# Running the next sequence's scores inside this sequence's softmax waits, in a paged latent-attention decode

## The reference, cut to what matters

```python
past_ckv = cache_ckv[page_table].reshape(db, -1, MLA_KV_RANK)     # (8, 2048, 256)
past_kpe = cache_kpe[page_table].reshape(db, -1, MLA_ROPE)        # (8, 2048, 64)
...
sp = (jnp.einsum('bqhr,bkr->bhqk', ql, past_ckv)
      + jnp.einsum('bqhd,bkd->bhqk', qp, past_kpe)).astype(F32) * MLA_SCALE
p = jax.nn.softmax(jnp.concatenate([sp, s], axis=-1), axis=-1).astype(ckv.dtype)
o = (jnp.einsum('bhqk,bkr->bqhr', p[..., :n_past], past_ckv)
     + jnp.einsum('bhqk,bkr->bqhr', p[..., n_past:], kc))
```

## Time and profile before

| | |
|---|---|
| median of three runs | 3417.89 us |
| the profiled execution | 3417.0 us, of which 3415.5 us are the span |
| PE busy | 3048.7 us, 89% of the span |
| DVE, ACT busy | 1380.2 and 1381.0 us, 40% each |
| POOL busy | 75.0 us, 2% |
| decode stage | 2702.8 us (first score) to 2839.6 us, 137 us or 4% of the span |

### The profile page before, as it was taken

The page is one execution under the profiler, slowest core; times in us unless marked ns, Lnnn a source line. Parts: engine busy times, 40 slices in busy tenths (PEclk is TensorE's granted clock), DMA queues, the critical chain, the costliest instruction groups (busy, mean ns, idle before and its releaser), DMA issues.

```text
span 3415.5 us, 56169 instructions
## 1 busy us (share of the span) xinstructions
PE 3048.7 (89%) x22503; PEld 2451.9 (72%) x22503; DVE 1380.2 (40%) x2522; ACT 1381.0 (40%) x1830; POOL 75.0 (2%) x139
## 2 busy tenths in 40 slices
PE   5999977899899979899997999978899668989996
PEld 3887866787678857788786887866555446778875
DVE  2334237777455452543325343222233213344322
ACT  3554346555322243655336553332222113455433
POOL 0000000000000000000000000000000120000000
PEclk8999988999899989999998999989999777999998
DMA  5223431122122224122331224421100474322221
GB/s 214 86 87 114 176 121 63 57 75 74 40 78 83 78 92 163 62 98 104 143 147 52 96 87 155 152 80 45 37 37 18 160 278 165 135 74 98 91 85 59
DMA packets 52952, 346.68 MB, mean 102 GB/s; under 512 B 7345, under 2 KB 7682, under 8 KB 23170
## 3 DMA queue, kind: packets, MB, share of 16 engines
q1 hardware_dynamic: 41906, 299.78, 24.5%
q0 software_dynamic: 10960, 45.71, 3.7%
HBM read 333.01 MB, written 12.45 MB: 101 GB/s over the span
## 4 chain that ended last, share of the span: by engine, by line
PE 82%; DVE 8%; ACT 4%; DVEq 2%; issue 2%; DMA 1%; ACTq 1%; SPq 0%; POOL 0%; PEldq 0%
PE PS L765 19%; PE PS L764 18%; PE PS L766 16%; PE PS L746 9%; PE PS L778 2%; PE PS L906 2%; PE PS L1102 1%; PE PS L1103 1%; PE PS L1115 1%; PE PS L1082 1%; PE PS L1090 1%; PE PS L1157 1%; DMA weight_ring<-in_ada_w 1%; PE PS L1132 1%; PE PS L786 1%
## 5 line engine op out<-in xcount | busy, mean ns | idle before, releaser
L764 PE MATMUL PS<-hid_hi,w_hi 128*128 128x260 f32 x2816 | 1012.8, 367 | 36.5 <-DVE hid_rest L1603 36.2
L765 PE MATMUL PS<-hid_rest,w_bf 128*128 128x260 bf16 x2816 | 806.2, 286 | 0.0
L1567 DVE TENSOR_TENSOR w_rest<-weight_ring,w_hi 128x1024 bf16<-128x1024 f32 (+1 forms) x304 | 363.6, 1197 | 1046.0 <-ACT w_hi L1257 1045.8
L766 PE MATMUL PS<-hid_bf,w_rest 128*128 128x260 bf16 x2816 | 775.6, 275 | 0.0
L1256 ACT ACTIVATE w_bf<-weight_ring 128x1024 bf16<-128x1024 f32 (+1 forms) x304 | 314.3, 1034 | 957.0 <-PE PS L766 954.9
L764 PEld LDWEIGHTS PS<-hid_hi,w_hi 128*128 128x128 f32 x2816 | 538.8, 191 | 83.8 <-issue 47.1
L764 PE MATMUL PS<-gu_hi,w_hi 128*128 128x260 f32 x1408 | 507.0, 367 | 5.6 <-DVEq L503 5.6
L765 PE MATMUL PS<-gu_rest,w_bf 128*128 128x260 bf16 x1408 | 403.1, 286 | 0.0
L766 PE MATMUL PS<-gu_bf,w_rest 128*128 128x260 bf16 x1408 | 387.6, 275 | 0.0
L765 PEld LDWEIGHTS PS<-hid_rest,w_bf 128*128 128x128 bf16 x2816 | 271.1, 96 | 114.7
L1257 ACT ACTIVATE w_hi<-weight_ring 128x1024 fp32r<-128x1024 f32 (+1 forms) x304 | 309.8, 1019 | 0.0
(11 more groups left out here) (380 smaller groups left out, 4302.7 us busy)
## 6 DMA issues: line engine op xcount, KB each, us to landing
weight_ring<-in_ffn_gu SPq DMA_DIRECT2D x88, 1024.0 KB, 4.8
ada_chunks<-in_ada_w SPq DMA_DIRECT2D x40, 1536.0 KB, 6.4
weight_ring<-in_ffn_wd SPq DMA_DIRECT2D x32, 1408.0 KB, 5.9
weight_ring<-in_w_hgrn SPq DMA_DIRECT2D x16, 1024.0 KB, 5.0
weight_ring<-in_ada_w SPq DMA_DIRECT2D x8, 1536.0 KB, 8.6
weight_ring<-in_w_ssm SPq DMA_DIRECT2D x8, 1536.0 KB, 6.4
weight_ring<-in_mla_pairs SPq DMA_DIRECT2D x8, 1536.0 KB, 6.3
arena<-in_pages SPq DMA_DIRECT2D x36, 288.0 KB, 5.5
```

The source lines that it names most:

```text
L764: pe.matmul(out, w_hi[:, buf, cols], hi[:, first + k, half], start=start and k == 0, stop=False)
L765: pe.matmul(out, w_bf[:, buf, cols], rest[:, first + k, half], start=False, stop=False)
L766: last = pe.matmul(out, w_rest[:, buf, cols], bf[:, first + k, half], start=False, stop=stop and k == n - 1)
L1567: tt(WL_[:, buf, 0:n], W[:, slot, j * DC * P:j * DC * P + n], WH[:, buf, 0:n].bitcast(F32), ALU.subtract).then_inc(w_rest_ready, 1)
```

## The change

The scores of a sequence become a function `scores(b2, bb, quarter)` of their own. PE computes sequence 0's scores before the loop, and `decode` of sequence b issues the four quarters of sequence b + 1 at three places: quarters 0 and 1 behind the transposes of b, quarter 2 behind the values of b, quarter 3 behind the sum of b's denominators. The wait for the pages of b + 1 stands ahead of quarter 0.

Exponentials are taken with each partition's own maximum (bias `DST[:, 3:4]`), so ACT starts them on `b_m`. The common maximum is still formed, beside that. A factor exp(scale x (own maximum - common maximum)), `DST[:, 9:10]`, one small ACT instruction, then multiplies the partition's sum and, together with the reciprocal, its part of the result. DVE's stream is rewritten as `own_max`, `combine` and `queries`; in `combine(b)` stand `own_max(b + 1)` and `queries(b + 2)`. The page loads in the streams of SP and POOL and the rule for `k_free` are as they were. Lines are shifted by the change: L1132 of before is L1134 of the changed kernel, L1150 is L1153, L1157 is L1164, L1979 is L2012.

```diff
@@ tensor stream @@
+                def scores(b2, bb, quarter):
+                    if quarter == 0:
+                        pe.wait_ge(b_q, b2 * 2 + (bb + 1))
+                        pe.wait_ge(k_in[bb % 2], b2 * (8 * NPAGE) + 8 * NPAGE * (bb // 2 + 1))
+                        pe.wait_ge(k_in_odd[bb % 2], b2 * (8 * NPAGE) + 8 * NPAGE * (bb // 2 + 1))
+                    for part in range(4):
+                        for q in range(QUARTERS):
+                            page = PAGES[bb % 2][4 * q + quarter]
...
+                    if quarter == 3:
+                        own = PS[0:QR_, 1, 0:NB]
...
-                    pe.wait_ge(b_m, b * 2 + 1)
+                    pe.wait_ge(b_m, b + 1)
                     pe.matmul(PS[0:1, 2, 0:P], DST[:, 2:3], IDENT, start=True, stop=True).then_inc(b_mt, 1)
-                    pe.wait_ge(b_m, b * 2 + 2)
-                    pe.matmul(PS[:, 3, 0:1], ROW[:, QR_:QR_ + P], ONES[0:1, 0:1], start=True, stop=True)\
-                        .then_inc(b_mt, 1)
                     pe.wait_ge(b_ex, b + 1)
                     for j in range(4):
                         pe.transpose(PS[:, 4, j * P:(j + 1) * P], PD[:, j, :], IDENT)
                     pe.transpose(PS[0:NB, 5, 0:QR_], PDO, IDENT[0:QR_, 0:QR_]).then_inc(b_pt, 1)
-                    pe.wait_ge(b_sum, b + 1)
-                    pe.matmul(PS[:, 7, 0:1], const("fold"), DST[:, 6:7], start=True, stop=True).then_inc(b_tot, 1)
+                    if more:
+                        scores(b2, bb + 1, 0)
+                        scores(b2, bb + 1, 1)
+                    pe.wait_ge(b_row, b + 1)
+                    pe.matmul(PS[:, 3, 0:1], ROW[:, QR_:QR_ + P], ONES[0:1, 0:1], start=True, stop=True)\
+                        .then_inc(b_bc, 1)
                     pe.wait_ge(b_ptc, b + 1)
...
                     pe.matmul(PS[0:QR_, 6, 0:RC * P], PTO, CKVS.rearrange("p a b -> p (a b)"),
                               start=False, stop=True).then_inc(b_o, 1)
+                    if more:
+                        scores(b2, bb + 1, 2)
+                    pe.wait_ge(b_sum, b + 1)
+                    pe.matmul(PS[:, 7, 0:1], const("fold"), DST[:, 6:7], start=True, stop=True).then_inc(b_tot, 1)
+                    if more:
+                        scores(b2, bb + 1, 3)
                     pe.wait_ge(b_on, b + 1)
...
+                for quarter in range(4):
+                    scores(0, 0, quarter)
+                with pe.Fori(0, NB // 2 - 1) as b2:
                     for bb in range(2):
-                        decode(b2, bb)
+                        decode(b2, bb, True)
+                for bb in range(2):
+                    decode(NB // 2 - 1, bb, bb == 0)
@@ scalar stream @@
-                        act.wait_ge(b_mx, b + 1)
+                        act.wait_ge(b_m, b + 1)
...
+                        act.wait_ge(b_all, b + 1)
+                        act.activation(DST[:, 9:10], DST[:, 2:3], ACT.Exp, bias=DST[:, 8:9], scale=SCALE).then_inc(b_w, 1)
                         act.wait_ge(b_o, b + 1)
                         act.sem_inc(k_free[bb], 1)
@@ vector stream @@
+                def own_max(b):
+                    dve.wait_ge(b_sc, b + 1)
+                    tt(PDO, PS[0:QR_, 1, 0:NB], const("own", QR_)[:, bass.ds(b * NB, NB)], ALU.add)
                     dve.reduce_max(DST[:, 0:1], PS[:, 0, :], AX_X)
...
+                    tt(DST[:, 2:3], DST[:, 0:1], DST[:, 1:2], ALU.max)
+                    dve.drain()
+                    ts(DST[:, 3:4], DST[:, 2:3], -SCALE, None, ALU.mult)
+                    dve.drain().then_inc(b_m, 1)
+                def combine(b, left):
+                    dve.wait_ge(b_mt, b + 1)
...
+                    dve.wait_ge(b_bc, b + 1)
+                    dve.tensor_copy(DST[:, 8:9], PS[:, 3, 0:1]).then_inc(b_all, 1)
                     dve.wait_ge(b_ex, b + 1)
...
+                    dve.wait_ge(b_w, b + 1)
+                    tt(DST[:, 6:7], DST[:, 6:7], DST[:, 9:10], ALU.mult).then_inc(b_sum, 1)
                     dve.wait_ge(b_tot, b + 1)
                     dve.reciprocal(DST[:, 7:8], PS[:, 7, 0:1])
                     dve.drain()
+                    tt(DST[:, 7:8], DST[:, 7:8], DST[:, 9:10], ALU.mult)
+                    dve.drain()
                     dve.wait_ge(b_o, b + 1)
+                    ts(OP, PS[:, 6, 0:RC * P], DST[:, 7:8], None, ALU.mult)
+                    dve.drain().then_inc(b_on, 1)
+                    if left > 1:
+                        own_max(b + 1)
+                    if left > 2:
+                        queries(b + 2)
                     dve.wait_ge(b_oc, b + 1)
```

More of the change, by code:

```diff
@@ L485, in build_program @@
         b_mt = sem("b_mt")
+        b_bc = sem("b_bc")
+        b_row = sem("b_row")
+        b_all = sem("b_all")
+        b_w = sem("b_w")
         b_sum = sem("b_sum")
@@ L1117, in head_pair @@
                         last.then_inc(p_o, 1)
-                def decode(b2, bb):
-                    b = b2 * 2 + bb
[L1122 to L1141, removed]
-                    pe.wait_ge(b_m, b * 2 + 1)
@@ new lines, in scores @@
+                def scores(b2, bb, quarter):
[6 more added lines that the diff above has]
+                            page = PAGES[bb % 2][4 * q + quarter]
+                            out = PS[q * QR_:(q + 1) * QR_, 0, quarter * PAGE:(quarter + 1) * PAGE]
+                            if part < RC:
+                                pe.matmul(out, QLB[:, part, :], page[:, part * PAGE:(part + 1) * PAGE],
+                                          start=(part == 0), stop=False)
+                            else:
+                                half = part - RC
+                                pe.matmul(out[:, half * 64:half * 64 + 64], QPB[:, half, :],
+                                          page[:, 4 * PAGE:4 * PAGE + 64], start=False, stop=(half == 1))
+                    if quarter == 3:
+                        own = PS[0:QR_, 1, 0:NB]
+                        for r in range(RC):
+                            pe.matmul(own, QLB[:, r, :], CKV[:, r, NP_:T], start=(r == 0), stop=False)
+                        pe.matmul(own, QPB[0:ROPE, 0, :], KPE[0:ROPE, NP_:T], start=False, stop=True).then_inc(b_sc, 1)
@@ L1144, in decode @@
+                def decode(b2, bb, more):
+                    b = b2 * 2 + bb
+                    pe.wait_ge(b_m, b + 1)
                     pe.matmul(PS[0:1, 2, 0:P], DST[:, 2:3], IDENT, start=True, stop=True).then_inc(b_mt, 1)
-                    pe.wait_ge(b_m, b * 2 + 2)
-                    pe.matmul(PS[:, 3, 0:1], ROW[:, QR_:QR_ + P], ONES[0:1, 0:1], start=True, stop=True)\
-                        .then_inc(b_mt, 1)
                     pe.wait_ge(b_ex, b + 1)
@@ L1953, in mla, with queries @@
                 dve.drain()
-                with dve.Fori(0, NB) as b:
+                def queries(b):
                     dve.tensor_copy(QLB[:, :, 0:MH], QL[:, :, :, b])
@@ L1969, in mla @@
                     ts(ROW[:, QR_:QR_ + P].rearrange("p (a b) -> p a b", a=QUARTERS),
[L1970 to L1972 removed]
+                       bcast(ROW[:, 0:QR_], 1, QUARTERS), -SCALE, None, ALU.mult).then_inc(b_row, 1)
+                    dve.wait_ge(b_bc, b + 1)
+                    dve.tensor_copy(DST[:, 8:9], PS[:, 3, 0:1]).then_inc(b_all, 1)
                     dve.wait_ge(b_ex, b + 1)
[L1974 removed]
+                    tt(DST[:, 6:7], DST[:, 4:5], DST[:, 5:6], ALU.add)
+                    dve.drain()
+                    dve.wait_ge(b_w, b + 1)
+                    tt(DST[:, 6:7], DST[:, 6:7], DST[:, 9:10], ALU.mult).then_inc(b_sum, 1)
                     dve.wait_ge(b_tot, b + 1)
@@ L1977, in mla @@
                     dve.drain()
+                    tt(DST[:, 7:8], DST[:, 7:8], DST[:, 9:10], ALU.mult)
+                    dve.drain()
                     dve.wait_ge(b_o, b + 1)
-                    ts(OP, PS[:, 6, 0:RC * P], DST[:, 7:8], None, ALU.mult).then_inc(b_on, 1)
+                    ts(OP, PS[:, 6, 0:RC * P], DST[:, 7:8], None, ALU.mult)
[4 more added lines that the diff above has]
+                        queries(b + 2)
                     dve.wait_ge(b_oc, b + 1)
                     dve.tensor_copy(OL[:, :, :, b], PS[:, 7, MH:MH + RC * MH].rearrange("p (a b) -> p a b", a=RC))
+                queries(0)
+                own_max(0)
+                queries(1)
+                with dve.Fori(0, NB - 2) as b:
+                    combine(b, 3)
+                for b in range(NB - 2, NB):
+                    combine(b, NB - b)
                 fence()
```

6 lines of the change are left out of this document (1 added, 5 removed).

## The result

| | before | changed kernel |
|---|---|---|
| median of the runs of this comparison | 3417.36 us (4 runs) | 3451.57 us (4 runs, 3449.79 to 3452.69) |
| ratio | | 1.0098, 95% interval 1.0080 to 1.0115 |
| span of the profiled execution | 3415.5 us | 3451.2 us |

The account below looks back on a forecast made before the run. Page load plus PE work was taken to bound the cycle: 16.4 + 0.1 + 5.8 = 22.3 us, six times; with sequence 0 1.6 late, sequence 7 10.6 and 1.0 behind it, + 27.2 us on 3417.89: 3445, range 3438 to 3452.

Parts of the forecast that it names:

- the circle through the DMA: Decode stage: page load, quarters 0 and 1, row matmul, values, `b_o`, next load; cycle 22.3 us, where it was 17.1.
- the free run of sequence 7: Last sequence waits for no pages and gets what the change promises: 10.6 us to its `b_o`.
- the softmax gain: Time taken from the softmax circle, such as 1.9 us before ACT's start, all spent in page waits of about 9 us.
- P: PE part of the cycle: quarters 0 and 1, row matmul, values, L1160's kind; 2.6 + 0.6 + 2.0 + 0.6 = 5.8 us.
- L: One sequence's page load, from `b_o` to the last DMA engine done: mean 16.4 us, range 15.8 to 16.9.
- wake of the wait: In each cycle, added between load and PE work: 0.1 us.
- half clock throughout: Rival: PE may not see full clock before `b_o`; P 7.2, cycle 23.7, total 3455 us; chance 0.18.
- The pages come in time: Rival: softmax circle sets the cycle, 12.2 us, total 3385; chance 0.05 for a gain, 0.04 for no change (3418).
- A shorter load: Rival: PE and DVE quieter while pages arrive; L 14.5, cycle 20.4, total 3434 us; chance 0.13.

Follow-up runs that it names:

- The wait alone: Kernel before, with PE also waiting for the pages of sequence b + 1 ahead of the values of b, nothing moved: 3443.93 us, ratio 1.0071, cycle 21.3 us.
- kept busy: Changed kernel with 13 useless matmuls on PE ahead of the wait for pages in sequences 1, 3 and 5: 3445.6 us (one run), cycle 22.2 us.

## Why the prediction was right, step by step

**That the circle through the DMA decides: right.** It named the place (the wait ahead of the values), the closing (`k_free` on `b_o`), the six cycles and the free run of sequence 7. The wait alone in the kernel before reproduces about 25 of the 34 us, and taking pages away takes the cycle down with them.

**That the softmax gain is swallowed: right.** PE's waits for pages are 10.5 to 11.2 us; I said 9, since I put the end of the transposes at +7 and the pages at +16.5. The transposes ended at about +6 (2748.5 for the `b_o` at 2742.2) and the first score came at +17.1, and without loads the gain is there. ACT started its exponentials as said, 0.06 us behind DVE's last own-maximum instruction (2746.13 against 2746.07).

**The size: short by a fifth, 27.2 forecast, 34.2 measured between medians, and inside the range partly by luck.** In the profiled executions the stage, from SP's first page issue to the first instruction behind it on PE, is 38.2 us longer (2683.62 to 2875.22 against 2686.19 to 2839.56), while all that lies ahead of it took 2.6 us less in that execution and all behind it the same. Against 38.2 the terms are:

| term | forecast | measured | |
|---|---|---|---|
| load, `b_o` to first score | 16.5 | 17.06 | x 6 = + 3.4 us |
| P, first score to `b_o` | 5.8 | 6.72 | x 6 = + 5.5 us |
| `b_o` of 0, later behind SP's first issue by | 1.6 | 3.0 | + 1.4 us |
| `b_o` of 6 to `b_o` of 7 | 10.6 | 11.0 | + 0.4 us |
| behind `b_o` of 7, longer by | 1.0 | 1.3 | + 0.3 us |

Both terms of the cycle came out at or over the upper ends that I had given them: P is 6.45 to 6.88 us against 5.0 to 6.5, and the cycle is 23.8 us where the upper ends add up to 23.5. (The stated ends are also a little narrow: L = 15.8 with P = 5.0 gives 3436 and not 3438, L = 16.9 with P = 6.5 gives 3453 and not 3452.) With the stage longer by 38.2 and all else equal the total would have been 3456, outside the 3438 to 3452 of the forecast. The time ahead of the stage differs from execution to execution, whatever the kernel: over the twelve traces SP's first page issue lies between 2682.1 and 2689.3 us. That the medians gave 3451.6, 0.4 us inside the range, is luck in this part; the mechanism is not.

The load's transfer was sized nearly right, 16.5 to 16.7 us to the last data in five loads of the changed kernel against L = 16.4, but "0.1 (wake of the wait)" was wrong. Three windows of the changed kernel show it: data still moving, its last window, and PE's first:

```profile
2780.00:2781.00 1.00, 0.00 (x0) 0.00 (x0) 0.00 (x0) 0.00 (x0) 0.00 (x0) 0.50 1.05 394
2782.20:2782.40 0.20, 0.00 (x0) 0.00 (x0) 0.00 (x0) 0.00 (x0) 0.00 (x0) 0.50 0.09 35
2783.00:2783.20 0.20, 0.18 (x4) 0.18 (x8) 0.00 (x0) 0.00 (x0) 0.00 (x0) 0.50 0.00 0
```

From the end of the last window with data to the first matmul it is 0.6 us here (2782.4 to 2783.02) and 0.5 to 0.7 in four other loads; the windows are 0.2 us long. In the trace of before only sequence 0 let PE wait for a landing, and there the next load was moving behind it, so its end could not be read.

P was too short in the values: I let one or two of eight steps run at half clock and came to 2.0 us. In the six cycles they took 2.61, 2.78, 2.86, 2.95, 2.93 and 3.03. The full clock came in the middle of the values or later: in the cycle shown the granted clock was 0.50 up to 2764.0, 0.78 in the next microsecond and 1.00 in the one after, with the values from 2762.58 to 2765.37. The rest of P is small: the two quarters up to the row matmul took 2.8 us and not 2.6, the row matmul 0.5 and not 0.6. I had the earlier trace rows, where the fourth quarter of sequence 0 was still mostly at half clock after a long idle time, and gave more weight to sequence 2, which had idled for 1.3 us only. The rival "half clock throughout" (P = 7.2, 3455) had the direction of this right, and it was the nearer of the two: P = 6.7 is 0.5 from its 7.2 and 0.9 from my 5.8, and 3451.6 is 3.4 from its 3455 and 6.6 from my 3445. I had given it 0.18 and the forecast 0.60.

**The rivals.** "The pages come in time": decided at L = 11.3 by my reckoning; the load stayed at 16.6, 17.1 with the wake. Its circle, 12.2 forecast, was 12.0 in the kernel without loads. "A shorter load": PE and DVE were idle for most of the load and it got no shorter, 16.6 us against 16.4. The factor (L1497, of unknown price before) took 0.30 us each and lies beside the values, as said:

```profile
L1497 ACT ACTIVATE arena<-arena x8: 278/295/296, 2715.8 to 2867.5; 128x1 f32<-128x1 f32 x8
```

## What to carry to other kernels

When work of the next item is pulled into the waits of this one, look at what its own waits stand in front of on an engine that works in order. If the thing it waits for is a load into a double buffer, and behind it in the queue is the work that frees a buffer, the load is no longer hidden but becomes part of the cycle, even where the wait lists of before show no wait for it; compare load time with the distance from freeing to first use, not with idle time. Put the early work behind the release, and split the wait so that each piece asks only for its own data: the same idea then gave 1.1% where it had cost 1.0%.

## What the runs showed of the hardware that I had not expected

- From the last data of a load to the first matmul that waited for it: 0.5 to 0.7 us in five loads of the changed kernel.
- The load of 4.72 MB took 16.4 us from `b_o` to its last data with PE at work beside it and 16.5 to 16.7 us with PE idle for most of it. Halving the pages brought the time to the first score from 17.1 to 11.1 us, not to half. If the moved pages are priced alike, about 5 us of both do not go with their number (an estimate, 17.1 less twice 6.0). 0.9 of them lie ahead of SP's first issue and 0.5 to 0.7 behind the last data; the rest is not divided by any run here.
- P of one and the same chain of matmuls was 4.2 us behind unbroken PE work, at a granted clock of 1.00 (kept busy, sequence 1), and 5.9 to 6.9 us behind an idle time of 10 to 11 us, which it began at 0.50.
- How long a stretch of PE work runs at half clock behind an idle time is not the same from cycle to cycle: the same 32 value products took 2.61 to 3.03 us in six cycles of one execution.
